# Retention in a two-layer decoder step: the transposes of keys and outputs as crossbar DMAs, the carried state placed in PSUM

## The reference, cut to what matters

```python
def step(s, qkv):                       # one chunk of 128 tokens, all heads
    qc, kc, vc = qkv
    scores = jnp.einsum('bihd,bjhd->bhij', qc, kc) * intra[None]
    o = jnp.einsum('bhij,bjhe->bihe', scores, vc)
    o = o + jnp.einsum('bihd,bhde->bihe', qc, s) * q_decay[None, :, :, None]
    s = s * chunk_decay[None, :, None, None] + jnp.einsum(
        'bjhd,bjhe->bhde', kc * k_decay[None, :, :, None], vc)
    return s, o
...
    mu = jnp.mean(o, axis=-1, keepdims=True)
    var = jnp.mean(jnp.square(o - mu), axis=-1, keepdims=True)
    o = ((o - mu) * lax.rsqrt(var + GN_EPS)).reshape(...)
    y = (jax.nn.silu(h @ w_g) * o) @ w_o
```

## Time and profile before

| | us |
|---|---|
| median of 3 runs (lowest to highest) | 2066.98 (2063.63 to 2071.34) |
| the profiled execution | 2069.52 |
| its span, on the slowest core (core 6) | 2068.5 |
| spans of the eight cores | 2046.2 to 2068.5 |

### The profile page before, as it was taken

One profiled execution on the slowest core, in us unless ns is written; L12 is line 12 of the kernel. 1 busy time (PEld: TensorE's weight loads), 2 busy tenths in 40 slices (PEclk: granted clock), 3 DMA queues, 4 the chain that ended last, 5 costly groups with the idle time before them and its releaser, 6 DMA issues.

```text
span 2068.5 us, 30269 instructions; the slowest of 8 cores (2046.2 to 2068.5 us)
## 1 busy us (share of the span) xinstructions
PE 1900.4 (92%) x10512; PEld 874.2 (42%) x10512; DVE 901.2 (44%) x1538; ACT 711.6 (34%) x1132; POOL 171.9 (8%) x363
## 2 busy tenths in 40 slices
PE   4899999999989899999988998899999988899997
PEld 1444444343434333334434444445454532454553
DVE  2555443434335853433556665332222457422224
ACT  2554543312226652123343443221012466310112
POOL 0011111010001000000001111010000000010000
PEclk9999999999999999999999999999999988999999
DMA  8313334798976248878534333453324230134342
GB/s 190 59 40 61 72 62 87 200 196 185 204 179 132 36 97 210 188 190 223 142 106 85 75 64 70 100 84 62 64 52 82 47 62 1 31 59 82 53 74 92
DMA packets 87252, 211.92 MB, mean 102 GB/s; under 512 B 10784, under 2 KB 13728, under 8 KB 84000
## 3 DMA queue, kind: packets, MB, share of 16 engines
q0 software_dynamic: 35952, 114.08, 33.9%
q1 hardware_dynamic: 51152, 95.90, 14.7%
HBM read 277.10 MB, written 48.89 MB: 158 GB/s over the span
## 4 chain that ended last, share of the span: by engine, by line
PE 73%; DVE 9%; DMA 8%; issue 5%; ACT 4%; DVEq 0%; SPq 0%; POOL 0%; ACTq 0%; POOLq 0%
PE ps L576 72%; DMA S_2_110<-st_in 2%; DMA wr<-wa 2%; DVE rt L604 2%; PE ps L581 1%; DMA x_62<-xTp 1%; DMA S_0_108<-st_in 1%; ACT sq L592 1%; DMA S_3_111<-st_in 1%; DVE rec_130 L607 1%; DMA x_63<-xTp 1%; ACT rec_129 L592 1%; DVE stat L833 1%; DVE rec_129 L607 1%; DVE h_45 L607 1%
## 5 line engine op out<-in xcount | busy, mean ns | idle before, releaser
L576 PE MATMUL ps<-h_44,wr 128*128 128x512 bf16 x1824 | 418.6, 385 | 15.3 <-DMA wr<-wa 6.1
L576 PE MATMUL ps<-h_45,wr 128*128 128x512 bf16 x1824 | 417.6, 383 | 6.3 <-ACT s_105 L592 3.0
L576 PEld LDWEIGHTS ps<-h_44,wr 128*128 128x128 bf16 x1824 | 176.1, 99 | 233.7 <-issue 39.3
L576 PEld LDWEIGHTS ps<-h_45,wr 128*128 128x128 bf16 x1824 | 174.7, 98 | 226.5 <-issue 31.3
L256 POOL DMA_DIRECT2D wr<-w x152 | 80.7, 532 | 1069.3 <-PE ps L576 941.9
L576 PE MATMUL ps<-aT_104,wr 128*128 128x512 bf16 x704 | 160.6, 381 | 0.9 <-DVE aT_137 L604 0.7
L576 PE MATMUL ps<-aT_106,wr 128*128 128x512 bf16 x704 | 159.8, 379 | 0.0
L592 ACT ACTIVATE s_105<-ps 128x512 f32<-128x512 f32 x88 | 52.3, 596 | 303.8 <-PE ps L576 277.9
L604 DVE TENSOR_TENSOR aT_106<-s_107,ps 128x512 bf16<-128x512 f32 x88 | 60.4, 687 | 219.5 <-PE ps L576 193.8
L604 DVE TENSOR_TENSOR aT_104<-s_105,ps 128x512 bf16<-128x512 f32 x88 | 60.4, 687 | 216.2 <-PE ps L576 184.4
L576 PE MATMUL ps<-wr,h_44 128*128 128x512 bf16 (+1 forms) x576 | 127.9, 370 | 5.2 <-ACT rstd_58 L592 2.2
(11 more groups left out here) (296 smaller groups left out, 2249.2 us busy)
## 6 DMA issues: line engine op xcount, KB each, us to landing
wr<-w POOLq DMA_DIRECT2D x88, 512.0 KB, 7.0
wr<-wa POOLq DMA_DIRECT2D x24, 1024.0 KB, 10.3
wr<-w POOLq DMA_DIRECT2D x64, 352.0 KB, 7.4
wr<-wo POOLq DMA_DIRECT2D x16, 512.0 KB, 8.1
S_0_108<-st_in SPq DMA_DIRECT2D x16, 512.0 KB, 8.9
S_1_109<-st_in SPq DMA_DIRECT2D x16, 512.0 KB, 6.2
S_2_110<-st_in SPq DMA_DIRECT2D x16, 512.0 KB, 7.3
S_3_111<-st_in SPq DMA_DIRECT2D x16, 512.0 KB, 6.7
```

What stands on the lines that cost most here:

```text
L576: self.S.op("pe", lambda e: e.matmul(out, lhsT, rhs, start=start, stop=stop, skip_group_check=skip), r, w, dur=k * max(0.1, self.n(out) * ...
```

## The change

The PE transposes of the prompt's keys and outputs, and the ACT copies behind them, are taken out. In their place SyncE issues DMA transposes from SBUF to SBUF: for the keys one for each half `a` of 128 rows and all four chunks, right behind the rotation of that half; for the outputs one for each chunk, right behind the ACT operation that writes `u`. `r_tl` and its pieces are gone. In pass 1, `first_state` copies the carried state by VectorE into banks 4 and 5 (for the first head after two matmuls that write all columns of the banks), the matmuls of `r_su` accumulate on it, and the bf16 state is made by an ACT copy in both passes. The last three pieces of the last `P` are held back and stand ahead of `wo_p(0)`, whose last two pieces now follow the merged part.

```diff
+    def dma_tr(self, out, in_, r, w, sem):
+        self.S.op("sp", lambda e: e.dma_start_transpose(out, in_), r, w, dsem=sem, nbytes=256 * self.n(in_))
...
-    def gn_gate(self, ob, obb, eps_ap, g_ap, gb, on, onb, u, ub):
+    def gn_gate(self, ob, obb, eps_ap, g_ap, gb, on, onb, u, ub, post=None):
...
-        return self.defer([sb2, onb], lambda: self.act(u, on, AF.Copy, [onb, sb2], [ub], scale=st[:, 8:9]))
+        def fin():
+            self.act(u, on, AF.Copy, [onb, sb2], [ub], scale=st[:, 8:9])
+            if post:
+                post()
+        return self.defer([sb2, onb], fin)
...
                         half_rope(0)
+                        if which == 1:
+                            ktr(0)
                         def second():
                             half_rope(1)
+                            if which == 1:
+                                ktr(1)
...
-            def ktr(c):
-                def fn():
-                    bk, bb = self.pb(DN)
-                    bv = bk.bitcast(BF16)
-                    for a in range(2):
-                        self.tr(bv[:, a * 128:(a + 1) * 128], k[p][0][:, a, c * 128:(c + 1) * 128], [k[p][1][a]], [bb])
-                    self.act(kt[p][0][:, c, :], bv[:, 0:256], AF.Copy, [bb], [kt[p][1][c]])
-                return (1, fn, self.need(k[p][1], pool=DN))
+            def ktr(a):
+                self.dma_tr(kt[p][0][:, :, a * 128:(a + 1) * 128], k[p][0][:, a, :], [k[p][1][a]], [kt[p][1][a]], f"kt{p}{a}")
...
             for c in range(4):
-                pcs.append(ktr(c))
                 pcs.append(vg("g", c))
...
-            gnj[n % 2] = self.gn_gate(ob, obb, ..., u[:, i, :], ub[i])
+            self.force(gnj[i])
+            post = lambda: self.dma_tr(uT[ti][0][:, h * 4:(h + 1) * 4, c * 128:(c + 1) * 128], u[:, i, :], [ub[i]], [uTb[ti][h][c]], f"ut{n % 4}")
+            gnj[i] = self.gn_gate(ob, obb, ..., u[:, i, :], ub[i], post)
...
-                self.mm(ps[:, 4 + a, :], kt[...], v[p][0][:, c, :], ci == 0, ci == 7, ...)
+                self.mm(ps[:, 4 + a, :], kt[...], v[p][0][:, c, :], s == 0 and ci == 0, ci == 7, ...)
...
-                if s == 0:
-                    self.act(sb_[:, :, :], S2, AF.Copy, sbk, sbb)
-                else:
-                    si_, sib = Sin[h % 2]
-                    self.tt(sb_[:, :, :], S2, si_[:, :, :], ALU.add, sbk + sib, sbb)
+                self.act(sb_[:, :, :], S2, AF.Copy, sbk, sbb)
...
-                    self.tt(si_[:, :, :], S2, si_[:, :, :], ALU.add, sbk + sib, sib)
-                    self.act(si_[:, :, :], si_[:, :, :], AF.Copy, sib, sib, scale=float(np.exp(GL[h] * OFFS)))
+                    self.act(si_[:, :, :], S2, AF.Copy, sbk, sib, scale=float(np.exp(GL[h] * OFFS)))
...
         def first_state(h, n):
             if s == 1:
-                self.act(Sbf[n % 2][0][:, :, :], Sin[h % 2][0][:, :, :], AF.Copy, Sin[h % 2][1], Sbf[n % 2][1])
+                si_, sib = Sin[h % 2]
+                for a in range(2):
+                    if h == 0:
+                        self.mm(ps[:, 4 + a, :], cb[:, CB_ID:CB_ID + 128], cb[:, CB_QM:CB_QM + 512], True, True, [cbb], [self.bank[4 + a]])
+                self.vcopy(ps[:, 4:6, :], si_[:, :, :], sib, [self.bank[4], self.bank[5]])
+                self.act(Sbf[n % 2][0][:, :, :], si_[:, :, :], AF.Copy, sib, Sbf[n % 2][1])
...
-        def r_tl(n):
...
                 if ti == 0:
                     main = P(h, 1)
+                    if h == RH - 1:
+                        main, held = main[:-3], main[-3:]
...
-                    X.run([sc_piece(len(seq) - 4), tl_piece(len(seq) - 5)])
-                    main = wo_p(0, range(8))
+                    main = held + wo_p(0, range(6))
                 X.merge(main, Rp(h, ti))
-        X.run([tl_piece(len(seq) - 1)])
+        X.run(wo_p(0, (6, 7)))
+        for it in gnj:
+            self.force(it)
         X.run(wo_p(1, range(8)))
```

More of the change, by code:

```diff
@@ L869, in ret_layer @@
         k = [Ar.tile(f"k{i}", [128, 2, TT], BF16, 2) for i in range(2)]
-        kt = [Ar.tile(f"kt{i}", [128, 4, 256], BF16, 4) for i in range(2)]
+        kt = [Ar.tile(f"kt{i}", [128, 4, 256], BF16, 2) for i in range(2)]
         v = [Ar.tile(f"v{i}", [128, 4, 512], BF16, 4) for i in range(2)]
@@ L1053, in r_o @@
             e = CF_EC + ci * 4 + h
-            gnj[n % 2] = self.gn_gate(ob, obb, cf[:, e:e + 1], g[p][0][:, c, :], g[p][1][c], on[:, i, :], onb[i], u[:, i, :], ub[i])
+            self.force(gnj[i])
+            post = lambda: self.dma_tr(uT[ti][0][:, h * 4:(h + 1) * 4, c * 128:(c + 1) * 128], u[:, i, :], [ub[i]], [uTb[ti][h][c]], f"ut{n % 4}")
+            gnj[i] = self.gn_gate(ob, obb, cf[:, e:e + 1], g[p][0][:, c, :], g[p][1][c], on[:, i, :], onb[i], u[:, i, :], ub[i], post)
         def r_su(n):
@@ L1060, in r_su @@
             for a in range(2):
-                self.mm(ps[:, 4 + a, :], kt[p][0][:, c, a * 128:(a + 1) * 128], v[p][0][:, c, :], ci == 0, ci == 7,
-                        [kt[p][1][c], v[p][1][c]], [self.bank[4 + a]], skip=True)
+                self.mm(ps[:, 4 + a, :], kt[p][0][:, c, a * 128:(a + 1) * 128], v[p][0][:, c, :], s == 0 and ci == 0, ci == 7,
+                        kt[p][1][a:a + 1] + [v[p][1][c]], [self.bank[4 + a]], skip=True)
             S2 = ps[:, 4:6, :]
@@ L1113, in need_su @@
             p = par(h, ti)
-            return self.need([kt[p][1][c], v[p][1][c]], [bank[4], bank[5]])
+            return self.need(kt[p][1] + [v[p][1][c]], [bank[4], bank[5]])
         def sc_piece(n):
             return (0.5, lambda: r_sc(n), need_sc(n))
-        def tl_piece(n):
-            return (1, lambda: r_tl(n), self.need([ub[n % 2]], [bank[7]]))
         def Rp(h, ti):
@@ L1125, in Rp @@
                 n = (h * 2 + ti) * 4 + c
-                if c == 0 and not (h == RH - 1 and ti == 1):
+                if c == 0:
                     pcs.append(sc_piece(n))
@@ L1131, in Rp @@
                     pcs.append(sc_piece(n + 1))
-                if n >= 1 and n != len(seq) - 4:
-                    pcs.append(tl_piece(n - 1))
             return pcs
@@ L1177, in ret_layer @@
         uT_bufs(1)
+        held = []
         for h in range(RH):
```

## The result

| | before | after |
|---|---|---|
| median, us (lowest to highest) | 2068.74 (2063.63 to 2071.34) | 2091.80 (2085.11 to 2098.74) |
| ratio, 95% interval | | 1.0106 (1.0077 to 1.0136) |
| spans of the cores, us | 2046.2 to 2068.5 | 2039.4 to 2092.2 |

The forecast was 2030 us; what came is slower than the kernel before, and outside the range. In the highest run of the changed kernel, 2098.74 us, the cores of one die were slower than those of the other; the ratio leaves it out, and without it the range ends at 2093.22 us. First the cores of the changed kernel: span and granted clock of each.

The account below looks back on a forecast made before the run. PE, busy 92% of the span, was taken as the bound. Gains of 21.7 + 6.8 + 13.1 us less losses of 2, 1 and 1.6 us gave 37.0 us, from 2067.0 to 2030 us; range 2001 to 2063 us.

Parts of the forecast that it names:

- The sum of 37.0 us: Whole kernel: total forecast gain, 21.7 + 6.8 + 13.1 - 2 - 1 - 1.6 us.
- The bank 7 waits: Retention: PE's seven waits for ACT's copy to `uT` out of the shared bank go, worth 6.8 us.
- the carried state did no harm: Carried state and starts: copies into PSUM replace additions; only the first copy adds work, at most -1.6 us.
- `sT` waits: Retention: PE's waits for masked scores, 12.0 us in pass 0 and 15.4 us in pass 1; 13.1 us forecast to go.
- the start of `wo`: Output projection's start: PE stalls for late output transposes at landings from 3.5 or 5.2 us on; taken as -2 us.
- the 21.7 us of PE's queue: PE's queue: output and key transposes leave it, 64 x 0.23 + 64 x 0.11 us, called the surest term.
- the landing time: DMA transposes: each taken to land in 5 us, between 2.7 us from below and 13.2 us from above.
- so the keys are covered even at 13.2 us: Retention: a key half is first used 20.8 us after its rotation, so no key waits were expected.
- ACT's rewriting of `u`: Retention: ACT must wait for the transpose of two chunks earlier, a cover of 16 us; no loss counted.
- The contention term of -1 us: Shared DMA engines: weights land later beside transposes, costing -1 us (none to -3).
- The transposes become the bound: Rival: crossbar takes the 48 DMAs of a pass one after another; at 8 us each some 2319 us; chance 0.09.
- The waits take its place: Rival: no `sT` wait gained, `r_o` waits instead, at most 14.7 us come back; 2071 us, chance 0.08.

Follow-up runs that it names:

- the pair with thin loads: Changed kernel and kernel before, each with the retention's weight loads cut to a sixteenth of their columns: 2033.55 us (0.9816) and 2067.87 us (0.9989).
- the thinned kernel: Changed kernel with the retention's weight loads (qk, v, g, wo) cut to a sixteenth of their columns: 2033.55 us, ratio 0.9816.
- `u` in the gate's tile and four semaphores: Changed kernel with `u` written over the used-up gate chunk in place of a tile of two: 2131.54 us, ratio 1.0321.
- the run with eight semaphores: Changed kernel with `u` in the gate's tile and eight semaphores, not four, for the outputs' transposes: 2067.88 us, ratio 0.9997.

## Why the prediction was wrong

**What it gains was right in kind, and nearly in sum.** The sum of 37.0 us compares with 34.3 us in the pair with thin loads. The bank 7 waits went, and the carried state did no harm. Of the `sT` waits 13.1 us were forecast to go and 27.4 + 3.4 - 14.3 = 16.5 us went; the start of `wo` was to cost 2 us and cost 8.7 us with thin loads. That these two misses nearly cancel is luck. No single run isolates the 21.7 us of PE's queue.

**The step that failed is the landing time**: "I take 5 us, nearer to the row of the queue that will carry them, and leave some of it for the weight bursts". It set one landing for all 48, between 2.7 us and the 13.2 us that a weight load took in a burst, and took 13.2 us as the upper bound. Neither row shows a DMA that stands behind another queue's load. The measured landings are 2.3 us in the median for most transposes and 31 to 38 us in core 3's worst bursts, and only the worst matter. From this two losses follow, and a third term looked at the wrong side:

- "so the keys are covered even at 13.2 us" was true and no help. At 34.6 us the cover of 20.8 us is used up: 47.2 us of waits in place of none. The text asked when the keys are needed, not what POOL issues in the same microseconds; the loads' issue times were in the trace of before.
- ACT's rewriting of `u` had a cover of 16 us; with landings of up to 38.1 us it cost 88.0 us of ACT and 10.2 us of PE through `Sbf`, taken as none.
- The contention term of -1 us looked at the weights alone. They landed later (14.1 us in place of 10.3 us in the median), but PE's waits for them went only from 7.7 to 8.3 us, within the stated bounds; it was the transposes that suffered.

**A second step failed at the start of `wo`**, taken as -2 us: it cost 5.8 + 5.7 = 11.5 us, and 8.7 us even in the thinned kernel. The prediction let the 13th matmul, "the first that needs it", wait for the last chunk of tile 0. By the rows above, the waiting matmuls wait for chunks of tile 1, whose semaphores they share. In pass 0 tile 0 was not late: its last transpose, issued at 273.6 us, had landed by 283.1 us, and PE stalled from 285.6 us on.

47.2 + 10.2 + (11.5 - 2) = 67 us on core 3, against 37.0 + 23.1 = 60 us between the forecast and the measured medians: the failed terms are of the size of the miss. Thinning the loads shows it without a sum of waits: the ratio of the changed kernel falls from 1.0106 to 0.9816, some 60 us, and that of the kernel before only to 0.9989. That waits displace each other is the likely reason for the 7 us too much, which is argued and not shown here; with `u` in the gate's tile and four semaphores it is seen, as the slowest core waited 47.8 us for `Sbf` and only 3.0 us for `kt`.

**The rivals.** None was the right one. "The transposes become the bound" had the wrong mechanism: they do not queue on each other, and a pass has room for 48 landings of 2.5 us. Signs that fit it came true all the same (SP behind its own DMAs, a lower clock), though landings did not grow along a pass; signs alone don't prove a mechanism. "The waits take its place" named `sT`, not the DMAs.

The two pages of the Trainium skill can now be weighed. Advanced Engine Details and Errata, section X-Bar Transpose (TRN2), has such DMAs as fast as regular ones: the trace agrees, 19.7 us for the transposes and 20.8 us for the copies beside three loads. VectorE: DVE Perf Modes, section The three transpose paths, gives 1309 ns for a 128x128 block, by estimate 5.2 us for four; here a DMA of four blocks landed in 2.5 us alone, and the measurement decides.

## What to carry to other kernels

The cover of a moved transfer is to be held against its landing time in the worst company that it keeps, so list what else is issued within its flight, on every queue, before taking a median. Here small transfers with short rows suffered from large loads much more than the loads from them (2.5 to 7.5 us against 8.1 to 9.0 us beside one load); issue them before the loads, or leave on PE what is needed soon. A semaphore that several DMAs share makes a wait for one of them a wait for all: it cost ACT 134.9 us, GpSimd most of 85.4 us and PE at the start of `wo` 8.7 us in three of these runs. Gains and losses of a change can lie in different parts of it, and here they could be had apart: 1.8% faster in place of 1% slower.

## What the hardware showed that was not expected

- Rows of 512 bytes in a load of 1 MB cost it 9.4 us in place of 8.1 us by itself, and the step with three loads and four transposes up to 3.5 us more by core, while the four transposes landed in 8.6 us in place of 19.7 us (medians). Whether this pays in the kernel stays open.
- Eight cores with one program meet such contention differently: `kt` waits of 15.8 to 51.5 us by core in the run with eight semaphores. A median core would have hidden the loss.
- A stall of 21 us costs more than itself: the next eight matmuls ran at half the clock (3.62 us in place of 1.89 us).
